# Hybrid decoder step: the down projection with activations stationary and 512 columns of w_down streaming

## The reference, cut to what matters

```
x  = x + concat(a, p) @ w_out
h2 = rmsnorm(x, norm2_g)
x  = x + (silu(h2 @ w_gate) * (h2 @ w_up)) @ w_down      # D_MODEL 2048, D_FF 5632
y  = rmsnorm(x, norm_f_g)                                # y_prompt (256 rows), y_sample (32 rows)
```

## Time and profile before

| | us |
|---|---|
| median of 3 runs | 1498.43 |
| profiled execution, whole | 1500.12 |
| its span | 1498.3 |
| PE busy | 1413.0 (94%) |
| DVE busy | 889.7 (59%) |
| ACT busy | 503.2 (34%) |
| mean granted clock of TensorE | 0.977 |

### The profile page before, as it was taken

One profiled execution on the slowest core, in us unless ns is written; L12 is line 12 of the kernel. 1 busy time (PEld: TensorE's weight loads), 2 busy tenths in 40 slices (PEclk: granted clock), 3 DMA queues, 4 the chain that ended last, 5 costly groups with the idle time before them and its releaser, 6 DMA issues.

```text
span 1498.3 us, 34216 instructions
## 1 busy us (share of the span) xinstructions
PE 1413.0 (94%) x13918; PEld 1308.8 (87%) x13918; DVE 889.7 (59%) x1319; ACT 503.2 (34%) x666; POOL 109.1 (7%) x184
## 2 busy tenths in 40 slices
PE   6998999989787899999999999999999999999986
PEld 5987777767454689999999999999999999999986
DVE  4778777766665544774555464646464646464635
ACT  4322122212122323554333333333333333333333
POOL 2127500000000000310000000000000000000003
PEclk9999999999887999999999999999999999999998
DMA  5898999999996766655555555555555555555531
GB/s 181 265 330 281 383 400 401 401 395 396 388 370 235 225 208 204 194 164 165 167 168 167 164 162 166 168 168 165 164 162 167 168 167 163 165 164 167 168 127 64
DMA packets 164280, 334.42 MB, mean 223 GB/s; under 512 B 10223, under 2 KB 54440, under 8 KB 163599
## 3 DMA queue, kind: packets, MB, share of 16 engines
q1 hardware_dynamic: 164183, 333.06, 66.2%
HBM read 328.10 MB, written 5.27 MB: 223 GB/s over the span
## 4 chain that ended last, share of the span: by engine, by line
PE 81%; SPq 8%; DVE 5%; issue 2%; DMA 2%; ACT 1%; POOL 0%; POOLq 0%; ACTq 0%; DVEq 0%
PE banks L1383 24%; PE banks L1384 24%; PE banks L1385 23%; PE banks L1496 4%; SPq L411 3%; SPq L415 3%; DVE kpage L867 2%; PE banks L1389 2%; PE banks L1478 2%; SPq L433 2%; DMA vpage<-in_cache_v 2%; SPq L403 1%; DMA vec<-in_pool_scale 1%; PE banks L1562 0%; PE banks L1512 0%
## 5 line engine op out<-in xcount | busy, mean ns | idle before, releaser
L825 DVE TENSOR_TENSOR w_lo<-w_raw,w_hi 128x1024 fp32r<-128x1024 f32 x360 | 440.4, 1230 | 423.6 <-ACT w_hi L562 423.1
L1383 PE MATMUL banks<-hh,w_hi 128*128 128x288 f32 x2176 | 647.9, 298 | 9.7 <-DVE w_lo L825 6.5
L1384 PE MATMUL banks<-hl,w_hi 128*128 128x288 f32 x2176 | 646.7, 297 | 0.0
L1385 PE MATMUL banks<-hh,w_lo 128*128 128x288 f32 x2176 | 643.7, 296 | 0.7 <-issue 0.7
L562 ACT ACTIVATE w_hi<-w_raw 128x1024 fp32r<-128x1024 f32 x360 | 378.9, 1058 | 672.9 <-PE banks L1385 459.5
L1383 PEld LDWEIGHTS banks<-hh,w_hi 128*128 128x128 f32 x2176 | 412.4, 190 | 26.6 <-issue 23.8
L1384 PEld LDWEIGHTS banks<-hl,w_hi 128*128 128x128 f32 x2176 | 412.5, 190 | 1.4 <-issue 1.4
L1385 PEld LDWEIGHTS banks<-hh,w_lo 128*128 128x128 f32 x2176 | 411.4, 189 | 0.6 <-issue 0.6
L1383 PE MATMUL banks<-ah,w_hi 128*128 128x288 f32 x704 | 209.0, 297 | 9.5 <-DVE af L1239 5.4
L1385 PE MATMUL banks<-ah,w_lo 128*128 128x288 f32 x704 | 209.7, 298 | 0.0
L1384 PE MATMUL banks<-al,w_hi 128*128 128x288 f32 x704 | 209.4, 297 | 0.0
(11 more groups left out here) (182 smaller groups left out, 648.1 us busy)
## 6 DMA issues: line engine op xcount, KB each, us to landing
kpage<-in_cache_k SPq DMA_DIRECT2D x128, 512.0 KB, 7.8
vpage<-in_cache_v SPq DMA_DIRECT2D x128, 512.0 KB, 7.0
w_raw<-in_w_gate SPq DMA_DIRECT2D x88, 512.0 KB, 3.6
w_raw<-in_w_up SPq DMA_DIRECT2D x88, 512.0 KB, 3.6
w_raw<-in_w_down SPq DMA_DIRECT2D x88, 512.0 KB, 3.7
w_raw<-in_w_in SPq DMA_DIRECT2D x64, 512.0 KB, 9.6
w_raw<-in_w_out SPq DMA_DIRECT2D x32, 512.0 KB, 4.3
xs<-in_x_prompt SPq DMA_DIRECT2D x2, 1024.0 KB, 7.4
```

The lines of the kernel that those rows point to most:

```text
L825: V.tensor_tensor(w_lo[:, s, :], w_raw[:, s, :], w_hi[:, u, :].bitcast(F32), ALU.subtract).then_inc(lo_ready, 1)
L1383: PE.matmul(o, wh, xh[:, c, :], start=start and i == 0, stop=False)
L1384: PE.matmul(o, wh, xl[:, c, :], start=False, stop=False)
L1385: last = PE.matmul(o, wl, xh[:, c, :], start=False, stop=stop and i == len(chunks) - 1)
```

## The change

In the down projection the activations become the stationary operand and w_down streams. Each round has now, for each of its four 128-row chunks k and for both halves p of the 256 prompt tokens, three matmuls `ah x w_hi`, `al x w_hi`, `ah x w_lo` with 128 stationary token columns and 512 streaming columns, summed by token in one bank per half. The 32 sample tokens are one plain fp32 matmul per chunk: `af` (not split) stationary with 32 columns, the raw tile `w_raw` streaming, and chunk k goes to the 32-row quarter k of a third bank. Both tiles of a round are counted as used only behind these four.

So that the raw tile survives, the low part of down tiles goes to a buffer of its own, `d_lo` with four slots. `af` gets four buffers instead of two, and `mul_act` loses its wait on them. The residual is held by token in `yt`: in group 0 DVE turns `xT` in 36 blocks of 32 tokens by 16 x 32 features, three behind each of 12 `lo`; the sample rows of `yt` start at zero, with the turned residual of the 32 sample tokens in its first quarter, and collect one partial sum per quarter. Each round ends with three adds of 128x512 (sample, prompt half 0, half 1) in place of four of 128x288. The wait for the earlier stores moves from the end to ahead of group 0, on SP and DVE, and SP issues five DMAs there that spread the last gain over the partitions (1.25 MB in the buffers).

In the last group PE folds the four sample quarters by one fp32 matmul for each round (`fold_sample`). ACT squares and sums by row, DVE multiplies by the gain and scales in SBUF, and y is stored in eight DMAs. The transposes, POOL's third sum of squares and the sums over partitions at the end are gone.

```diff
@@ block.sync
+            sp.wait_ge(stored, 16 * STORES)
+            gf = A["norm_f_g"].unsqueeze(0)
+            sp.dma_start(gfin[:, :], gf.to_broadcast([P, D])).then_inc(gain_in, 16)
+            for c in range(4):
+                sp.dma_start(gsam[32 * c:32 * c + 32, :], gf[:, 512 * c:512 * c + 512].to_broadcast([32, 512])
+                             ).then_inc(gain_in, 16)
             with sp.Fori(0, NG - 1) as g:
...
@@ block.vector
-            def lo(t):
+            def lo(t, apart=False):
                 n, _, s, u = t
                 dve.wait_ge(hi_ready, n + 1)
-                V.tensor_tensor(w_lo[:, s, :], w_raw[:, s, :], w_hi[:, u, :].bitcast(F32),
+                V.tensor_tensor(d_lo[:, u, :] if apart else w_lo[:, s, :], w_raw[:, s, :], w_hi[:, u, :].bitcast(F32),
                                 ALU.subtract).then_inc(lo_ready, 1)
...
+            def turn_residual(a, b):
+
+                part, b = b // 4, b % 4
+                V.transpose(yt[32 * b:32 * b + 32, part, :].rearrange("t (c f) -> t c f", c=KC)[:, :, 32 * a:32 * a + 32],
+                            xT[32 * a:32 * a + 32, :, P * part + 32 * b:P * part + 32 * b + 32]).then_inc(res_turned, 1)
+
+            def add_down(quad, c, used, signal):
+
+                dve.wait_ge(w_used, used)
+                for p in (2, 0, 1):
+                    y = yt[:, p, 512 * c:512 * c + 512]
+                    V.tensor_tensor(y, y, bank[4 * quad + p][:, :], ALU.add).then_inc(signal, 1)
+
+            def group(g):
                 for k in range(24):
-                    lo(tile_at(T_FF + 12 + k, g, 24))
+                    lo(tile_at(T_FF + 12 + k, g, 24), 12 <= k < 20)
...
                     if k >= 16 and k % 2 == 1:
                         c = (k - 17) // 2
-                        add_group((c + 1) % 2, 4 * c, T_FF + 24 + 24 * g + 2 * c + 2)
+                        if isinstance(g, int) and c == 0:
+                            dve.wait_ge(res_turned, len(blocks_) + 2)
+                        add_down((c + 1) % 2, c, T_FF + 24 + 24 * g + 2 * c + 2, quad_taken[(c + 1) % 2])
+                    if isinstance(g, int) and k < 15 and k != 7:
+                        for a, b in blocks_[3 * (k - (k > 7)):3 * (k - (k > 7)) + 3]:
+                            turn_residual(a, b)
...
@@ block.tensor
+            def fold_sample(c):
+
+                pe.wait_ge(y_added, 3 * c + 1)
+                PE.matmul(bank[3][32 * c:32 * c + 32, :], fold[:, :], yt[:, 2, 512 * c:512 * c + 512], start=True,
+                          stop=True).then_inc(folded, 1)
...
                     for j in range(2):
                         if c == 0:
                             pe.wait_ge(act_ready, 4 * g + 2 * j + 2)
-                        w_tile(tile_at(*((t0[0] + 2 * c + j,) + t0[1:])), 512, (2 * j, 2 * j + 1),
-                               bank[4 * quad:4 * quad + 4], ah, al, j == 0, j == 1)
+                        pe.wait_ge(lo_ready, ts[j][0] + 1)
+                        for i in range(2):
+                            k, (wh, wl, _) = 2 * j + i, moved(j, i)
+                            for p in range(2):
+                                rows = slice(P * p, P * p + P)
+                                PE.matmul(out[p][:, :], ah[:, k, rows], wh, start=k == 0, stop=False)
+                                PE.matmul(out[p][:, :], al[:, k, rows], wh, start=False, stop=False)
+                                PE.matmul(out[p][:, :], ah[:, k, rows], wl, start=False, stop=k == 3)
+
+                    for k in range(4):
+                        ins = PE.matmul(out[2][32 * k:32 * k + 32, :], af[:, k, TP:T], moved(k // 2, k % 2)[2],
+                                        start=True, stop=True)
+                        if k % 2:
+                            ins.then_inc(w_used, 1)
+                    if last and c:
+                        fold_sample(c - 1)
```

More of the change, by code:

```diff
@@ L546, in _ @@
             load_down((T_END - 8,), NG - 1)
[L547 to L552, removed]
+            for p in range(2):
+                for e in range(2):
+                    sp.wait_ge((fy_act, fy_dve)[e], 2 * p + 2 + p * e)
+                    store(O["y_prompt"][0, p * P:(p + 1) * P, 1024 * e:1024 * e + 1024],
+                          yt[:, p, 1024 * e:1024 * e + 1024])
+                if p == 0:
+                    sp.wait_ge(fy_dve, 3)
+                    for c in range(4):
+                        store(O["y_sample"].rearrange("b q d -> (b q) d")[:, 512 * c:512 * c + 512],
+                              ys[32 * c:32 * c + 32, :])
             sp.wait_ge(stored, 16 * n_stores)
@@ L809, in _ @@
             act.wait_ge(rf_ready, 1)
[L810 to L814, removed]
+            for p in range(2):
+                for c in range(2):
+                    y = yt[:, p, 512 * c:512 * c + 512]
+                    copy_by(y, y, rf[:, p:p + 1]).then_inc(fy_act, 1)
         @block.vector
@@ new lines, in _ @@
+            dve.wait_ge(stored, 16 * STORES)
+            gate_scaled(0)
+            up_scaled(0)
+            V.memset(yt[:, 2, :], 0.0).then_inc(res_turned, 1)
+            V.tensor_reduce(fold[:, :], ident.rearrange("p (k i) -> p i k", k=4), AX.X, ALU.add).then_inc(res_turned, 1)
+            dve.wait_ge(res_turned, 2)
+            V.tensor_copy(row_of[:, :, :], fold[:, :].unsqueeze(1).to_broadcast([P, 4, 32])).then_inc(fold_ready, 1)
+            group(0)
+            with dve.Fori(1, NG - 1) as g:
+                group(g)
@@ L1264, in _ @@
             for k in range(12):
[L1265 removed]
+                lo(tile_at(T_END - 12 + k), k >= 4)
                 if k == 7:
                     mul_act(NG - 1)
[L1269 to L1277, removed]
[L1278 to L1285 removed]
@@ L1287, in _, with gained_y @@
-            dve.wait_ge(sq_summed, 3)
-            for n in range(3):
-                rows = P if n < 2 else TS
-                V.tensor_scalar(fm[0:rows, n:n + 1], bank[4 + n][0:rows, 0:1], 1.0 / D, EPS, ALU.mult,
-                                ALU.add).then_inc(fms, 1)
+            own.did(V.memset(fm[:, :], 1.0))
+            dve.wait_ge(gain_in, 80)
+            def gained_y(p, c):
+                y = yt[:, p, 512 * c:512 * c + 512]
+                dve.wait_ge(y_squared, 2 * c + p + 1)
+                V.tensor_tensor(y, y, gfin[:, 512 * c:512 * c + 512], ALU.mult).then_inc(y_gained, 1)
@@ new lines, in _ @@
+            for c in range(4):
+                add_down(c % 2, c, T_END - 8 + 2 * c + 2, y_added)
+                if c:
+                    for p in range(2):
+                        gained_y(p, c - 1)
+            dve.wait_ge(folded, 4)
+            V.tensor_copy(ys[:, :], bank[3][:, :]).then_inc(ys_taken, 1)
+            dve.wait_ge(y_squared, 8)
+            own.link(V.tensor_reduce(rf[:, 0:2], fq[:, 0:8].rearrange("p (n c) -> p n c", n=2), AX.X, ALU.add))
+            own.link(V.tensor_scalar(fm[:, 0:2], rf[:, 0:2], 1.0 / D, EPS, ALU.mult, ALU.add))
@@ L1366, in _ @@
             sum_squares(1)
-            sum_squares(2)
         @block.tensor
@@ L1779 @@
+                 (None, (act_ready, 4 * NG), (y_added, 3), (y_added, 6)), last=True)
+            fold_sample(3)
+            pe.wait_ge(ys_squared, 1)
+            PE.matmul(bank[7][:, 0:1], row_of[:, :, :].rearrange("p k i -> p (k i)"), fq[:, 8:9], start=True, stop=True).then_inc(ys_summed, 1)
 STORES = 4 + 1 + 1 + NB
```

115 lines of the change are left out of this document (57 added, 58 removed).

## The result

| | before | after |
|---|---|---|
| median of runs, us | 1498.62 (1497.38 to 1501.32, 4 runs) | 1525.46 (1523.55 to 1527.78, 4 runs) |
| ratio, 95% interval | | 1.0177 (1.0165 to 1.0190) |
| profiled execution, whole | 1500.12 | 1526.50 |
| its span | 1498.3 | 1524.7 |
| granted clock, mean | 0.977 | 0.976 |

The change makes the kernel 26.8 us slower. The forecast was 1520, slower, with 1505 to 1530 as the range. One execution of all that follow, one of e8's eight, took 5695 us: e8's median of 1494.55 counts it and is 1494.15 without it, and its ratio leaves it out.

A forecast was written before the change was run, and what follows sets the result against it. PE's own time was taken to bound the kernel: 17.8 (ten groups) + 1.6 + 1.3 + 0.7 + 0.9 (last group) - 0.4 (end) = +21.9 us on the median 1498.43, forecast 1520, range 1505 to 1530.

The forecast's parts named there:

- PE's own time bounds the stage: Feed-forward stage: PE busy 50 of 50 us at clock 1.00, so the change is worth what it does to PE's time.
- Period 0.230 between 0.225 and 0.235: Down projection: a 512-column fp32r matmul starts every 0.230 us, from 0.225 (overhead per instruction) to 0.235 (proportional to columns).
- rival B: Down projection: only the fixed overhead, 512 columns take 0.216 us; +10.4 us, 1509; chance 0.25.
- rival E: Down projection: the instruction sets the period, 512 columns take the 0.132 us of 288; faster, 1475; chance 0.05.
- Samples 1.22 us a round: Down projection: the four sample matmuls with entering and leaving add 1.22 us per round, of which 0.85 is streaming.
- Round 1 by DVE's chain, 6.90: Second round of a group: late tile release makes DVE's chain to round 0's add take 6.90 us, 0.16 over PE's round.
- Ten groups +17.8: Ten groups' down parts: 3 x 6.74 + 6.90 = 27.12 us each, +1.78 per group, +17.8 us.
- Last group +4.5: Last group: rounds +1.6, longer wait ahead of round 2 +1.3, half clock +0.7, fold_sample(1) +0.9 us.
- The extra 0.7 for the half clock: Last group, behind the gap ahead of round 2: PE loses a further 0.7 us (0 to 1.7) at the half clock.
- End -0.4: From the last matmul to the end: first store at 8.8 instead of 9.0 us, taken as -0.4 us (-3 to +2).
- Costed at nothing: the transposes: Group 0: DVE's 36 residual transposes take 2.94 us per tile with lo against PE's 3.17, so cost 0.
- rival C: Group 0: DVE late, as strided transposes take 1.20 us each; a tile step 4.74 against 3.17; 1537; chance 0.07.

The follow-up runs named there:

- e8: Kernel before, with the last group's adds of rounds 0 and 1 moved behind lo 9 and 11: 1494.55 us, ratio 0.9962.
- e1: Changed kernel without the four sample matmuls of each down-projection round (y_sample lacks that term): 1488.58 us, ratio 0.9923.
- e5: Changed kernel with up_scaled behind lo 15 in place of lo 16: 1525.27 us, ratio 1.0181.
- e11: Changed kernel without the sample matmuls, and with up_scaled moved from behind lo 16 to directly behind gate_scaled: 1474.49 us, ratio 0.9837.
- e4: Changed kernel with the 36 residual transposes of group 0 spread over 15 lo instead of 12: 1524.73 us, ratio 1.0165.
- e12: Changed kernel without the 36 residual transposes, two memsets in their place (y lacks the attention's residual): 1522.06 us, ratio 1.0155.
- e13: Changed kernel with 8 of the 36 transposes ahead of group 0 and two behind each of 14 lo: 1523.72 us, ratio 1.0171.
- e9: Changed kernel with samples paired across rounds, up_scaled earlier, last group's adds earlier, 8 transposes before group 0: 1507.71 us, ratio 1.0060.

## Why the prediction was right, and where it was not

1. **PE's own time bounds the stage.** Right: PE works 49.87 of 50 us, and e1, which only shortens PE's work, is faster by 37 us.
2. **Period 0.230 between 0.225 and 0.235.** Measured 0.2319, 0.8% over; rival B's 0.216 is out, and with it 1509. The Trainium skill (TensorE: Matmul & The Clock Gate, "Back-to-back issue gap") has N/2.4 + 2.5 ns for isolated matmuls, which is 215.8 ns here, an estimate; the traces have 16 more. The 131 ns that the Trainium skill's same section has for 512 columns in real kernels (rival E) are nowhere; 132 is what 288 columns take.
3. **Samples 1.22 us a round.** Measured: 0.09 in, 0.99 for both waves and the way out, 0.11 for the exposed load: 1.19. The attention's rows were a good model of another line's instructions, since form and sizes agree.
4. **Round 1 by DVE's chain, 6.90.** Measured 6.96, and e5, e11 show that up_scaled is what makes it late.
5. **Ten groups +17.8.** Measured +19.5. Per group, in us: the period 0.0019 x 96 = +0.18, the samples -0.03 x 4 = -0.12, the wait +0.06, and the down part before was 25.28, not 25.34 (+0.06). None is a mistake in kind.
6. **Last group +4.5.** Measured +4.5, but the sum is partly luck. The rounds (+1.6) and `fold_sample(1)` (two records of 0.43, +0.9) came as forecast. The wait ahead of round 2 grew by 1.98 and not by 1.3: `fold_sample(0)` was put at nothing because it lies in the gap, but it ran at the half clock, 1.85 us, and outlasted the adds by about 0.6. The extra 0.7 for the half clock did not come: 32 matmuls of 288 columns at 0.108 lost 3.5 us before, 18 of 512 at 0.195 lose 3.5 now. That term could not be forecast so closely: last groups of the same code (after, e4, e12, e13) have 18, 12, 13 and 21 matmuls at the half clock and take 38.2, 36.7, 36.8 and 38.5 us, a scatter as large as the term.
7. **End -0.4.** Measured -0.2.
8. **Costed at nothing: the transposes.** This step failed, and PE waiting for `w_lo` in group 0 was one of the prediction's own signs of being wrong. The prediction set 3 x 0.60 + 1.14 = 2.94 us per tile against PE's 3.17. Measured is 3 x 0.73 + 1.26 = 3.46. Half of a 1024-element transpose's 1.20 is not what a 512-element one takes: the rows have 0.70 for one and 0.73 from start to start; and the saving of two `lo` in a row (1.14) does not hold between transposes, where a `lo` costs 1.26 (the `lo` at 688.91, behind a transpose but ahead of a product, costs 1.14). With a margin of 0.23 us per tile, an error of 0.52 turns cover into 0.29 of lateness per tile; the slack ahead of group 0 is used up by 683 us, and from there on PE pays. It is rival C in its mechanism, with 3.46 where C had 4.74: +4.2 us instead of +17. The forecast should have carried a part of C in its sum, as the margin was 7% on two durations that no row showed. The broadcasts did cost nothing (e12 keeps them, and shows 54.65).

Between forecast and ledger lie 4.6 us: 4.2 for point 8, 1.7 for point 5 and 0.2 for point 7, less 0.4 (first wait of the last group) and 1.2 (ahead of the stage), for which the prediction had no step.

## What to carry to other kernels

Turning a product round so that the wider operand streams cuts instructions, but not the time of a stream that is bound by its columns; ask first what the leftover rows (here 32 of 288 tokens) cost in a form of their own, for here they went from about 2.8 us per group to 4.6, where the rest gained 0.1. Work that is hidden "beside" an engine has to be costed by start-to-start distance of the same shape, and a cover within 10% of the limit belongs into the sum with a price. And look at the last turn of a loop written out by hand: an add that stands behind work for later rounds cost the kernel before 5 us, and moving it wins them back.

## What the runs showed of the hardware

- fp32r matmuls back to back at granted clock 1.00: 117.6 ns for 256 columns, 132.2 for 288, 231.9 for 512. A line through the last two is 4.0 ns and 0.445 ns per column, which gives 117.9 at 256; a fixed 12 ns on top of columns/2.4 would give 225 at 512 and 118.7 at 256, and is excluded. At the half clock 512 columns take 427, which is 512/1.2 with nothing on top; so what stands on top at full clock (10.9, 12.2 and 18.6 ns) grows with the columns, and no run here shows why.
- Each time PE stopped, the matmul after the next came 0.105 us late, even behind short waits: the six small waits in group 0 (0.14 to 0.18) cost 0.24 to 0.28 each with it. That this is the weight load with nothing to hide behind is the reading of these rows, not a separate experiment.
- Four 32-column quarters of fp32 by 512 columns take 0.43 us a wave. Two waves with entering and leaving cost 1.19 us; where the samples of two rounds stand together (e9), the pair costs 0.3 us less than two apart.
- A DVE transpose of 32x512 out of a strided tile takes 0.70 us, one of 128x1024 in place 1.20: more than half the time for half the elements per partition.
